# Two-layer attention block: the norms of heads c taken from squares summed by token, y split in six groups, the result stored in pieces

## What is computed

```python
def rms(x, w):
    y = x * lax.rsqrt(jnp.mean(x * x, axis=-1, keepdims=True) + EPS)
    return y * w
# heads c: 6 heads, 128 values without position + 64 with (QK_C = 192), v of 128
qc = rms(heads(rms(cq, qa_norm) @ w_qb, H_C), qn_c)
kvc = heads(rms(ckv, kva_norm) @ w_kvb, H_C)
kc = jnp.concatenate([kvc[..., :NOPE_C], broadcast(kpe)], axis=-1)
kc = rms(kc, kn_c)
vc = kvc[..., NOPE_C:]
# the last 64 values of qc and kc are rotated by position (latent tokens only)
o_c = softmax(qc @ kc.T * QK_C ** -0.5) @ vc        # latent: 256+256 keys; context: its 256 keys
# then y = concat(o_a, o_b, o_c) * silu(z), and x = x + gate * (y @ w_out)
```

## Time and profile before

| | |
|---|---|
| median of 3 runs | 3738.79 us (3736.97 to 3738.87) |
| the profiled execution, its own time | 3744.71 us |
| its span, first to last instruction | 3742.9 us, 61624 instructions |
| PE busy | 3486.1 us (93%) |
| DVE busy | 2128.9 us (57%) |
| ACT busy | 1458.0 us (39%) |
| heads c, layer 0: norm part from tile 13 to the first scores | 2550.0 to 2687.6 us |
| its attention, then the split of y | to 2746.0, to 2757.4 us |
| heads c, layer 1: the same | 3484.3 to 3589.5; to 3630.7, to 3637.3 us |
| out phase of layer 1, then the store | to 3732.8, to 3742.9 us |

### The profile page before, as it was taken

How to read it: one execution, slowest core, us unless ns; L and a number is a source line. 1 busy time by engine, 2 the same in 40 slices (tenths; PEclk the granted TensorE clock), 3 DMA queues, 4 the chain that set the end, 5 groups by cost and what they waited for, 6 DMA issues and landing times.

```text
span 3742.9 us, 61624 instructions
## 1 busy us (share of the span) xinstructions
PE 3486.1 (93%) x23040; PEld 2990.1 (80%) x23040; DVE 2128.9 (57%) x2954; ACT 1458.0 (39%) x2092; POOL 579.6 (15%) x542
## 2 busy tenths in 40 slices
PE   6997998899999999999999999998889899989878
PEld 6997997899987888878887787785567687868658
DVE  4566864556755555656565565537643464654754
ACT  4433443444433333343443525522332434463332
POOL 0295998011200000000300000000001000000000
PEclk9999998899999999999999999998899999999989
DMA  4553554355676767677722221121135433322214
GB/s 164 181 184 136 181 185 141 130 196 173 219 244 217 241 222 244 237 237 240 243 96 92 72 90 63 63 76 58 46 107 176 171 110 107 119 76 100 83 62 146
DMA packets 156886, 554.63 MB, mean 148 GB/s; under 512 B 17136, under 2 KB 21232, under 8 KB 156656
## 3 DMA queue, kind: packets, MB, share of 16 engines
q1 hardware_dynamic: 151680, 532.57, 41.5%
q0 software_dynamic: 4976, 18.88, 1.5%
HBM read 545.09 MB, written 6.29 MB: 147 GB/s over the span
## 4 chain that ended last, share of the span: by engine, by line
PE 70%; DVE 8%; POOLq 6%; POOL 5%; ACT 5%; issue 2%; DVEq 2%; DMA 1%; ACTq 0%; SPq 0%
PE psum L1639 20%; PE psum L1640 19%; PE psum L1641 19%; POOLq L2010 6%; POOL conv L2011 4%; PE psum L1669 4%; DVE rst L1084 2%; PE psum L1890 2%; PE psum L1916 2%; DVE wlo L1053 2%; PE psum L1737 1%; PE psum L1901 1%; ACT whi L701 1%; ACT probs L957 1%; DVE stat L1480 1%
## 5 line engine op out<-in xcount | busy, mean ns | idle before, releaser
L1639 PE MATMUL psum<-hcat,whi 128*128 128x256 f32 (+1 forms) x5516 | 1746.9, 317 | 69.4 <-DVEq L1042 30.7
L1641 PE MATMUL psum<-hcat,wlo 128*128 128x256 f32 (+1 forms) x5516 | 1714.6, 311 | 0.0
L1640 PE MATMUL psum<-hcat,whi 128*128 128x256 f32 (+1 forms) x5516 | 1714.3, 311 | 0.0
L1053 DVE TENSOR_TENSOR wlo<-raw,whi 128x1024 fp32r<-128x1024 f32 (+3 forms) x844 | 1031.7, 1227 | 838.7 <-ACT whi L701 802.0
L701 ACT ACTIVATE whi<-raw 128x1024 fp32r<-128x1024 f32 (+3 forms) x844 | 865.3, 1029 | 1239.3 <-PE psum L1641 854.3
L1639 PEld LDWEIGHTS psum<-hcat,whi 128*128 128x128 f32 x5516 | 1064.1, 193 | 201.4 <-issue 97.7
L1640 PEld LDWEIGHTS psum<-hcat,whi 128*128 128x128 f32 x5516 | 1064.9, 193 | 54.6 <-issue 3.8
L1641 PEld LDWEIGHTS psum<-hcat,wlo 128*128 128x128 f32 x5516 | 1063.5, 193 | 54.5
L2009 POOL TENSOR_SCALAR tap<-glu,par 128x255 f32<-128x255 f32 (+9 forms) x180 | 236.5, 1314 | 0.0
L1084 DVE RECIPROCAL rst<-rst 128x512 f32<-128x512 f32 (+1 forms) x65 | 181.2, 2787 | 41.9 <-ACT rst L722 41.9
L1639 PE MATMUL psum<-thirdcat,whi 128*128 128x256 f32 x687 | 201.0, 293 | 0.0
(11 more groups left out here) (179 smaller groups left out, 2958.6 us busy)
## 6 DMA issues: line engine op xcount, KB each, us to landing
raw<-in_stream SPq DMA_DIRECT2D x978, 512.0 KB, 4.2
raw<-in_stream SPq DMA_DIRECT2D x18, 384.0 KB, 2.9
raw<-in_stream SPq DMA_DIRECT2D x24, 256.0 KB, 2.5
X<-in_ctxT POOLq DMA_DIRECT2D x2, 2048.0 KB, 13.9
resid_dram<-X POOLq DMA_DIRECT2D x2, 2048.0 KB, 12.2
bias<-in_natten POOLq DMA_DIRECT2D x16, 256.0 KB, 3.0
X<-resid_dram POOLq DMA_DIRECT2D x2, 2048.0 KB, 9.3
raw<-in_stream SPq DMA_DIRECT2D x16, 192.0 KB, 2.4
```

The lines of the kernel that those rows point to most:

```text
L1053: vec.tensor_tensor(wlo[:, slot, 0:n], raw[:, slot, 0:n], whi[:, c % HI_SLOTS, 0:n].bitcast(F32), ALU.subtract).then_inc(lo_ready, 1)
L1639: pe.matmul(dst, h, cat[:, kk, c0:c0 + width], start=(q == 0 and k == 0), stop=False)
L1640: pe.matmul(dst, h, cat[:, kk, c0 + loff:c0 + loff + width], start=False, stop=False)
L1641: last = pe.matmul(dst, l_, cat[:, kk, c0:c0 + width], start=False, stop=(q == nq - 1 and k == nch - 1))
```

## The change

For heads c the twelve jobs of a layer go. ACT squares a tile as before (into a ring `csq` of four buffers; 16 squares a layer: kpe once, six k, nine q tiles), but PE now takes 128 tokens of the squares as the stationary operand and one or two columns of ones as the moving one, so that a sum stands by token: 128 tokens in the partitions, one column per block of 128. DVE then works on 8 columns instead of 512 (`mean_squares`): it adds, ACT takes the root (`col_root`), DVE the reciprocal. The factor of q, times the constant scale, goes into the exponential as a scale per query, and DVE's maxima multiply by its negative. The factor of k is spread again over the partitions by matmuls against the identity, two heads at a time (`spread`), and DVE scales k from that product (`scale_k`), with the weights of q and k multiplied into one. The rotated parts of q get their weight as they are copied from PSUM. The w_qb stream is put in another order (rotated part, then its two heads). The last items run beside the first two pairs of the attention. y is split in six groups, each as soon as its chunks of X are done; the first quarter of the first w_out tile waits for two groups only. The result is stored by SP in five pieces as its tiles get done.

```diff
@@ projections
-                for h, j in enumerate(JOBS_OF[f"kc{l}"]):
-                    at_(k0 + 3 + h, "sum", j, 0, 2)
-                    at_(k0 + 3 + h, "fin", j)
-                    at_(k0 + 1 + h, "sq", j, 0, 2, k0 + h)
+                n0 = CSQS * l
+                at_(k0, "csq", n0)
+                at_(k0 + 2, "col", n0)
+                for h in range(H_C):
+                    at_(k0 + 1 + h, "csq", n0 + 1 + h)
+                    at_(k0 + 2 + h, "col", n0 + 1 + h)
+                for g in range(3):
+                    at_(k0 + 3 + 2 * g, "kfin", g)
+                    at_(k0 + 4 + 2 * g, "spread", g)
...
-                for h, j in enumerate(JOBS_OF[f"qc{l}"]):
-                    t = q0_ + 3 + h
-                    at_(t + 2, "sum", j, 0, 2)
-                    at_(t + 2, "fin", j)
-                    if h % 2:
-                        at_(t + 3, "rope", ROPES_OF[f"qc{l}"][h // 2])
-                    at_(t + 1, "sq", j, 0, 2, t)
-            order = ("sum", "fin", "kpe", "rope", "vt", "cat", "sq")
+                for i in range(9):
+                    at_(q0_ + i + 1, "csq", n0 + 7 + i)
+                    at_(q0_ + i + 2, "col", n0 + 7 + i)
+                    if i % 3 == 0:
+                        at_(q0_ + i + 2, "rope", ROPES_OF[f"qc{l}"][i // 3])
+                    if i % 3 == 2:
+                        at_(q0_ + i + 2, "qfin", i // 3)
+            order = ("sum", "fin", "kpe", "rope", "vt", "cat", "col", "kfin", "spread", "qfin", "sq", "csq")
@@ vector
+            def mean_squares(l, g):
...
+                vec.wait_ge(csq_used, CSQS * l + heads[-1] + 1)
...
+                vec.tensor_tensor(st, own, other, ALU.add).then_inc(col_used, 1)
+                fence()
+                vec.tensor_scalar(st, st, 1.0 / QK_C, EPS, ALU.mult, ALU.add).then_inc(mean_sq_ready, 1)
+                vec.wait_ge(root_ready, n + 1)
+                if g < 3:
+                    vec.reciprocal(st, st).then_inc(rk_ready, 1)
+                else:
+                    vec.reciprocal(st, st)
+                    fence()
+                    for dst, f in ((q_factor, QK_C ** -0.5), (q_minus, -QK_C ** -0.5)):
+                        vec.tensor_scalar(dst[:, 2 * (g - 3):2 * (g - 3) + 2, 0:nb], st, f, None, ALU.mult)
+                    fence()
+            def scale_k(l, g):
+                vec.wait_ge(spread_ready, 3 * l + g + 1)
+                for h in range(2):
+                    k, a = cqk[:, KN + 2 * g + h, :], HD * h
+                    vec.scalar_tensor_tensor(k, k, qk_weight, psum[:, 7 - h, :], ALU.mult, ALU.mult)
+                    kr = cqk[a:a + HD, KR + g, :]
+                    last = vec.tensor_tensor(kr, kr, psum[a:a + HD, 7 - h, :], ALU.mult)
+                last.then_inc(spread_used, 1)
@@ vector, the attention of c
-                for p in range(len(us) + 3):
-                    if p < len(us):
+                for p in range(n + 3):
+                    if p < n:
                         maxima(us[p])
-                    if 1 <= p <= len(us):
+                    if p < len(carry):
+                        for_heads(carry[p], l)
+                    if 1 <= p <= n:
                         norms(us[p - 1])
                     if p >= 3:
                         gated(us[p - 3])
-                stage(f"y{l}")
-                four_lo(0, w, 4 * l)
-                stage(f"ycat{l}")
+                    for g in {n: (0,), n + 1: (1,), n + 2: (2, 3, 4, 5)}.get(p, ()):
+                        y_lo(l, g)
                 vec.wait_ge(resid_in, 48 if l else 32)
@@ scalar
+            def y_hi(l, g):
+                a, b = YCAT[g]
+                if g >= 3:
+                    us = PAIRS_OF[f"c{l}"]
+                    act.wait_ge(o_used, us[len(us) // 3 * (g - 2) - 1] + 1)
+                act.activation(hcat[:, a:b, 0:chunks_w(l)], X[:, a:b, 0:chunks_w(l)], ACT.Copy).then_inc(ycat_hi, 1)
+            def col_root(l, g):
+                act.wait_ge(mean_sq_ready, 6 * l + g + 1)
+                act.activation(col_stat[:, g, :], col_stat[:, g, :], ACT.Sqrt).then_inc(root_ready, 1)
...
+                    if 2 <= p < n + 2:
                         transposed(us[p - 2])
-                    if p < len(us):
+                    if p < n:
                         probabilities(us[p])
-                act.wait_ge(vector_stage, STAGE[f"y{l}"])
-                four_hi(0, w)
+                    for g in {n: (0,), n + 1: (1, 2, 3), n + 2: (4, 5)}.get(p, ()):
+                        y_hi(l, g)
@@ tensor
+                    elif it[0] == "col":
...
+                        for b in range(C["width"] // P):
+                            a = C["col"] + b
+                            last = pe.matmul(psum[:, col_bank(C["group"]), a:a + 4 * C["sel"].shape[-1]:4],
+                                             csq[:, n % 4, P * b:P * b + P], C["sel"], start=True, stop=True)
+                    elif it[0] == "spread":
...
+                        for h in range(2):
+                            for b in range(4):
+                                rk = col_stat[:, g, 4 * h + b:4 * h + b + 1].to_broadcast([P, P])
+                                last = pe.matmul(psum[:, 7 - h, P * b:P * b + P], rk, cv("ident"), start=True, stop=True)
...
-                pe.wait_ge(vector_stage, STAGE[f"ycat{l}"])
+                def y_ready(q):
+                    pe.wait_ge(ycat_lo, len(YCAT) * l + (2, len(YCAT))[q])
+                tile(C0[f"out{l}"], 0, T0[f"out{l}"], 0, hcat, 0, 2 * S, w, ready=y_ready)
@@ sync
+            done = [(0, 4), (4, 8), (8, 12), (12, 15), (15, 16)]
+            for a, b in done:
+                sp.wait_ge(x_tile, XT["out1"] + b)
+                sp.dma_start(out[:, a:b, :], X[:, a:b, 0:S]).then_inc(out_done, 16)
@@ gpsimd
-                pool.wait_ge(vector_stage, STAGE[f"ycat{l}"])
+                pool.wait_ge(ycat_lo, len(YCAT) * (l + 1))
                 pool.dma_start(X[:, :, 0:S], r).then_inc(resid_in, 16)
...
-            pool.dma_start(out, X[:, :, 0:S]).then_inc(out_done, 16)
```

More of the change, by code:

```diff
@@ L212 @@
 for _l in range(LAYERS):
-    STAGES += [f"{_s}{_l}" for _s in ("gains", "a", "b", "c", "y", "ycat", "out")]
+    STAGES += [f"{_s}{_l}" for _s in ("gains", "a", "b", "c", "out")]
 STAGE = {name: n + 1 for n, name in enumerate(STAGES)}
@@ L258, in build @@
     region("consts", CO["invcount"] * 4)
[L259 removed]
+    region("small", (96 * 2 + KD * 35 + 24 + LAYERS * H_B + S + 112) * 4)
     region("work", 16 * KIB)
@@ L473, in layer_jobs @@
             group(f"cq{l}", lambda: lora("cq", 0, 6, "qa_norm", hcat, 10))
[L475 to L493, removed]
         for l in range(LAYERS):
@@ L582, in projections, with col_bank @@
             return tiles_, [items.get(u, []) for u in range(steps)]
+        CSQS = 16
+        csqs = []
+        for l in range(LAYERS):
+            w_ = chunks_w(l)
+            csqs.append(dict(l=l, src=qkv[:, 10, :], sel=halves[:, 0:1], col=24, width=2 * S, group=0, tile=4, psum=False))
+            for h in range(H_C):
+                csqs.append(dict(l=l, src=cqk[:, KN + h, :], sel=ones[:, 0:1], col=4 * (h % 2), width=2 * S, group=h // 2,
+                                 tile=11 + h, psum=False))
+            for i in range(9):
+                t, m = i // 3, i % 3
+                if m == 0:
+                    csqs.append(dict(l=l, src=psum[:, BANK[T0[f"qb{l}"] + i], 0:w_], sel=halves[:, 0::HD],
+                                     col=40, width=w_, group=3 + t, tile=23 + i, psum=True))
+                else:
+                    csqs.append(dict(l=l, src=cqk[:, 2 * t + m - 1, 0:w_], sel=ones[:, 0:1], col=32 + 4 * (m - 1), width=w_,
+                                     group=3 + t, tile=23 + i, psum=False))
+        def col_bank(group):
+            return 5 - group % 2
+        YCAT = [(0, 4), (4, 8), (8, 10), (10, 12), (12, 14), (14, 16)]
+        tiles_of_c = [projections("c", l)[0] for l in range(LAYERS)]
         def copied(first, t):
@@ L927, in projected, with for_heads @@
                 return items[len(tiles_):]
-            def for_heads(todo, first):
-                for it in sorted(todo, key=lambda it: it[0] != "sq"):
+            def for_heads(todo, first, l):
+                for it in sorted(todo, key=lambda it: it[0] not in ("sq", "csq")):
                     if it[0] == "fin":
                         root(it[1])
+                    elif it[0] == "csq":
+                        n, C = it[1], csqs[it[1]]
+                        if n == CSQS * l:
+                            ckv = jobs[JOBS_OF[f"ckv{l}"][0]]
+                            act.wait_ge(cat_lo, ckv["cat0"] + len(ckv["cat"]))
+                        if C["psum"]:
+                            act.wait_ge(weights_used, tiles_of_c[l][C["tile"]][0] + SLOTS + 1)
+                        else:
+                            act.wait_ge(psum_free, copied(first, C["tile"]))
+                        if n >= 4:
```

(7 more changed lines are left out.)

179 lines of the change are left out of this document (121 added, 58 removed).

## The result

The changed kernel took **3655.78 us** (median of 4 runs, 3651.20 to 3658.16) against 3738.83 beside it on the same chip (4 runs): ratio 0.9775, 95% interval 0.9758 to 0.9791. The forecast was 3656, with a range of 3638 to 3690. The profiled execution took 3656.36 us, its span is 3654.6; that of before was 3742.9, so the traces differ by 88.3 us.

The account below looks back on a forecast made before the run. It took the norm parts, where PE waits behind DVE's wide reciprocals, as the main bound. Gains 44.1 + 32.5 + 0 + 0 + 6.0 = 82.6 us off the 3738.8 median gave 3656 us, range 3638 to 3690.

Parts of the forecast that it names:

- What bounded the kernel: Norm parts of heads c: PE and DVE take turns, PE waiting behind DVE's wide reciprocals, twelve taking 40.2 us.
- Norm part of layer 0: Tile 13 to first scores: 137.6 us falls to 93.5, gain 44.1; layer 1 from 105.2 to 72.7, gain 32.5.
- a column sum: Norm parts: one head of 512 tokens, four fp32 products on PE, priced at 0.95 us, 1.9 at the lower clock.
- DVE is late by 0.6 us in each of three rounds: k part of the norms: DVE needs 10.0 us per two tiles, PE 9.4; 1.8 us in all.
- The stage wait: End of the norm part: PE waits for the last copy and its drain, 1.3 us.
- Every link has a tile of lead: Norm chain through three queues: argument against rival B, that a tile of lead at each link keeps PE from waiting.
- rival B: In-order coupling in the norm chain: each of twelve `mean_squares` holds PE 2 to 3 us, 30 us lost, 3686; chance 0.2.
- The end of the norms in the attention: Two column sums and last q factor beside first pairs: table loads 2.6 us a layer against a warm PE; set at 0.
- The split of y: Before w_out: y ready 3.4 us earlier, early first quarter given back at the fourth; 0 for both layers, -5 to +10.
- The store: End of kernel: result in pieces, last piece landing in 2.4 us plus 1.4 to the end; gain 6.0, bounds 4 and 7.
- Rival C: Clock in the norm parts: PE stays at a mean of 0.85, 28 us more, 3684; chance 0.1.
- Rival D: Column sums overlap the tiles and the split keeps part of the quarters: 15 us better, 3641; chance 0.1.

Follow-up runs that it names:

- e6: Changed kernel with two unused 128x512 reciprocals put back on DVE in each `mean_squares` of the k groups: 3702.45 us, ratio 0.9909.
- e7: Changed kernel with two unused 128x512 reciprocals put back on DVE in each `mean_squares` of the q groups: 3691.33 us, ratio 0.9876.
- e11: The changed kernel itself, unedited, timed once more on another chip: 3649.93 us, ratio 0.9766.
- e5: Changed kernel with every column sum made twice: 3679.78 us, ratio 0.9845.
- e8: Changed kernel with the last q group's square root on ACT replaced by a square, needing no table switch: 3656.32 us, ratio 0.9785.
- e10: Changed kernel, six groups of y kept, but PE's first quarter of w_out waits for all six: 3640.10 us, ratio 0.9745.
- e1: Kernel before with only the store changed, issued in five pieces by SP: 3730.26 us against 3736.84, ratio 0.9984.
- e2: Changed kernel with y split as before, in ACT's four pieces after the last pair: 3647.83 us, ratio 0.9769.
- e12: Changed kernel with DVE's reload wait moved to first use, reload in halves, first w_out quarter waiting for all six y groups: 3637.82 us, ratio 0.9728.

## Why the prediction was right, and where

**What bounded the kernel: right.** The wide norms held PE through DVE, and without them PE sets the pace: 88.9 of 90.0 us busy. e6 and e7 put the reciprocals back, and each 39.8 us of them cost about 40 us or more.

**Norm part of layer 0, forecast 93.5 us, measured 90.0 (91.6 in e11); layer 1 72.7, measured 71.9 (70.3).** Right to 4%. Of the terms: a column sum was priced at 0.95 and spaced 0.80 (2.1 us less for 14); a spread 1.79, measured 1.78. "DVE is late by 0.6 us in each of three rounds", 1.8 us, was 0.3 in all. The stage wait, 1.3, was 0.8 in layer 0 and 2.5 in layer 1. In layer 0 these take 4.1 us off the forecast and leave 89.4. All work had been priced at the full clock, where the windows ran at 0.98 and 0.96; a stretch at the lower clock had no term. That the sums fill PE's time one for one is e5's result.

**"Every link has a tile of lead"**, said against rival B, was wrong as an argument, though B did not come to pass. By e6 the k chain's slack is about 0.75 us on average and none in the third group of layer 0. The kernel sat near the edge of B, not far from it.

**The end of the norms in the attention, forecast 0: right.** e8 gains 0.2 us a layer; the two loads hide beside PE's scores, but only just: e7 with 6.6 us more in the same place costs PE 6.7. The two column sums and the higher clock at the start, set against each other, come out near even: the last values start 58.3 us after the first scores in layer 0, with the granted clock at 1.00, and 58.0 in the kernel before, with 0.97 (layer 1: 40.0, and 41.7 in e11, against 40.8).

**The split of y, forecast 0: right in size, and in mechanism for layer 0.** PE "waits 7 to 8" before the fourth quarter: 6.42. "18.7 us after the split" for that quarter's low part, about 2 more for contention: 20.7 (2703.04 to 2723.70). 2 us to contention: 2.3, against e10. In layer 1 the wait was put at 5 us and was 8.84. There the text kept the reload wait of 9.78 us as it was; the load took 13.5 us from issue to release, 3.9 more than in e10, beside three loads of the stream. The text had all that e10 then showed: the first quarter is given back, with contention and a second restart. What it did not say is that leaving that quarter out would be faster than the change; the expectation of e10 put it at no difference. That step failed: it weighed the early quarter as a gain that is returned, where it is a loss.

**The store, forecast 6.0 (4 to 7), was 7.8 in the traces,** 6 by e1's median. Two parts were mis-sized: the last piece lands in 1.8 us, not 2.4, and from landing to end it is 0.4 us (3652.4 + 1.8 to 3654.6), where POOL's 1.4 had been taken.

**Rival C, the clock: fell.** PEclk is 0.98 and 0.95 in the norm parts, though one-column products stand between most tiles. In e5 it stays at 0.97 and 0.96 with twice as many. In e6 it falls to 0.88 and 0.89 with the waits. The falls follow waits of PE, not the kind of product. **Rival D fell too:** e5 shows that no column sum overlaps a tile, e2 that the split keeps nothing of the quarters.

The sum was 82.6 us, the traces show 88.3 of which 2.4 is scatter ahead of the change, the medians 83.05. Errors of 3.5, 0.8 and 1.8 us in one direction and 2.9 in the other, in the stretches behind the first scores; besides, the profiled execution of before lay 5.9 us above its median and that of the changed kernel 0.6. That the forecast came within 0.3 us of the median is partly luck.

**Left open:** why e10 and e12, whose traces agree in the stretches of the change to 0.6 us, have ratios 0.0017 apart. Their intervals overlap, and nothing in the profiles tells them apart.

## What to carry to other kernels

When a consumer is let in early, follow what it wants next: here the early first quarter only moved PE's stop to the fourth quarter, behind a wait at the head of DVE's in-order queue, and paid for a second restart; put such a wait at its first use, and test such edits together, since what one is worth depends on the other. Where a statistic needs few values, let TensorE put it by token, so that the vector engine works on 8 columns instead of 512. Measure the slack of the new chain by lengthening one step, not by its waits, which stand near zero whether the slack is large or small.

## What the runs showed of the hardware

- An fp32 product costs almost the same with one moving column as with 128: 8 instructions with one column take 0.80 us, 16 take 1.70; with 128 moving columns and a broadcast stationary operand 16 take 1.78, in which their weight loads are at work for 1.87 (PEld, first start to last end).
- A wait of 5.5 us of PE is followed by work at the lower clock: 3.43 us for what takes 1.78. With that, e6's waits of 35 us go with norm parts 47 us longer.
- The loads of residual and context in layer 0, 4 MB, reached DVE 16.7 us after the first one's issue where the stream's next load was issued 8.1 us after it (e10), and 19.0 where it was issued 3.5 us after it; the residual alone in layer 1 took 9.6 and 13.5.
- The exponential with a scale per partition takes 0.78 us for 512 columns, with a constant scale 0.68.
